# Second block's attention heads: the reciprocal softmax sums reach the head rows by DMA through DRAM instead of sixteen small products and a copy

## The reference, cut to what matters

```python
y = rmsnorm(h, norm_mix_g[l]) @ w_in[l]
q = partial_rotary(y[..., 0:512].reshape(B, S, 8, 64))
k = partial_rotary(y[..., 512:1024].reshape(B, S, 8, 64))
v = y[..., 1024:1536].reshape(B, S, 8, 64)
att = dilated_sliding_attention(q, k, v)      # softmax(q k^T / 8 + pattern) v, per head
conv = conformer_conv(...)                    # a convolution over 31 tokens, beside it
h = h + concatenate([att, conv]) @ w_out[l]
```

## Time and profile before

| | |
|---|---|
| median of three runs | 1579.19 us (1577.89 to 1580.6) |
| the profiled execution | 1579.18 us, its span 1576.9 us |
| PE busy | 1558.7 us, 99% of the span |
| DVE, ACT, POOL busy | 752.0, 627.4, 682.3 us |
| PE's granted clock | 0.99 of full speed over the whole, 1.00 in the stage of the change |
| attention stage, pairs 0 to 3 | 997.27 to 1046.21 us |

### The profile page before, as it was taken

One profiled execution on the slowest core, in us unless ns is written; L12 is line 12 of the kernel. 1 busy time (PEld: TensorE's weight loads), 2 busy tenths in 40 slices (PEclk: granted clock), 3 DMA queues, 4 the chain that ended last, 5 costly groups with the idle time before them and its releaser, 6 DMA issues.

```text
span 1576.9 us, 18796 instructions
## 1 busy us (share of the span) xinstructions
PE 1558.7 (99%) x7412; PEld 1261.0 (80%) x7412; DVE 752.0 (48%) x1295; ACT 627.4 (40%) x1135; POOL 682.3 (43%) x520
## 2 busy tenths in 40 slices
PE   9999999999999999999999999999999999999998
PEld 6888867788888888888888887568878888888886
DVE  6999523646666352133308698863432420022103
ACT  3534563543435333233332434673442542234322
POOL 1585333243544544454454454024413544444442
PEclk7999999999999999999999999999999999999999
DMA  9676532268534353333333442003213333333331
GB/s 319 139 110 154 134 81 80 54 227 281 202 104 134 110 171 126 96 98 94 105 109 99 135 120 81 14 28 94 81 40 94 102 99 97 103 89 99 96 104 68
DMA packets 221704, 180.28 MB, mean 114 GB/s; under 512 B 24232, under 2 KB 184360, under 8 KB 221488
## 3 DMA queue, kind: packets, MB, share of 16 engines
q1 hardware_dynamic: 214080, 166.68, 36.8%
q10 hardware_dynamic: 7536, 12.40, 2.2%
HBM read 172.49 MB, written 6.55 MB: 114 GB/s over the span
## 4 chain that ended last, share of the span: by engine, by line
PE 80%; ACT 1%; DVE 1%; POOL 0%; issue 0%; DVEq 0%; ACTq 0%
PE banks L647 13%; PE banks L648 13%; PE banks L653 13%; PE banks L729 9%; PE banks L730 9%; PE banks L734 9%; PE banks L776 3%; PE banks L759 1%; PE banks L760 1%; PE banks L761 1%; PE banks L1097 1%; PE banks L1110 1%; PE banks L1197 1%; PE banks L985 1%; PE banks L1183 0%; PE banks L1184 0%
## 5 line engine op out<-in xcount | busy, mean ns | idle before, releaser
L2564 POOL TENSOR_TENSOR w_lo<-raw,w_hi 128x512 fp32r<-128x512 f32 (+1 forms) x484 | 647.0, 1360 | 789.6 <-ACT w_hi L1267 788.8
L1267 ACT ACTIVATE w_hi<-raw 128x512 fp32r<-128x512 f32 (+1 forms) x484 | 275.9, 619 | 319.4 <-PE banks L734 244.7
L647 PE MATMUL banks<-h_hi,w_hi 128*128 128x512 f32 x936 | 367.1, 392 | 0.0
L648 PE MATMUL banks<-h_lo,w_hi 128*128 128x512 f32 x936 | 364.3, 389 | 0.0
L653 PE MATMUL banks<-h_hi,w_lo 128*128 128x512 f32 x936 | 250.2, 389 | 0.0
L647 PEld LDWEIGHTS banks<-h_hi,w_hi 128*128 128x128 f32 x936 | 175.7, 188 | 38.7 <-issue 2.4
L648 PEld LDWEIGHTS banks<-h_lo,w_hi 128*128 128x128 f32 x936 | 175.7, 188 | 36.6 <-issue 0.7
L653 PEld LDWEIGHTS banks<-h_hi,w_lo 128*128 128x128 f32 x936 | 175.7, 188 | 36.6
L2382 DVE SCALAR_TENSOR_TENSOR banks<-att_area,cols,banks 128x512 f32<-128x512 f32 x116 | 87.5, 754 | 3.4
L729 PE MATMUL banks<-w_hi,u_hi 128*128 128x512 f32 x224 | 87.1, 389 | 0.0
L730 PE MATMUL banks<-w_hi,u_lo 128*128 128x512 f32 x224 | 87.1, 389 | 0.0
(11 more groups left out here) (456 smaller groups left out, 2597.0 us busy)
## 6 DMA issues: line engine op xcount, KB each, us to landing
raw<-in_w_in SPq DMA_DIRECT2D x57, 512.0 KB, 4.2
raw<-in_w_ffn_up SPq DMA_DIRECT2D x44, 512.0 KB, 3.8
raw<-in_w_up SPq DMA_DIRECT2D x32, 512.0 KB, 4.0
raw<-in_w_down SPq DMA_DIRECT2D x32, 512.0 KB, 3.7
ada_ring<-in_w_ada SPq DMA_DIRECT2D x24, 512.0 KB, 5.7
raw<-in_w_ffn_down SPq DMA_DIRECT2D x20, 512.0 KB, 3.6
raw<-in_w_s_glu SPq DMA_DIRECT2D x16, 256.0 KB, 3.1
raw<-in_w_mlstm_down SPq DMA_DIRECT2D x8, 512.0 KB, 6.7
```

What stands on the lines that cost most here:

```text
L647: te.matmul(ps, wv[0][:, i, :], rh, start=(i == 0), stop=False)
L648: te.matmul(ps, wv[0][:, i, :], rl, start=False, stop=False)
L1267: sc.activation(W_HI[SLOT[key]][:, part_], raw[:, RAW_SLOT[key], part_], ACT.Copy).then_inc(*hi_set.up((key, n_)))
L2564: gp_.tensor_tensor(W_LO[s_][:, part_], raw[:, RAW_SLOT[key], part_], W_HI[s_][:, part_].bitcast(F32), ALU.subtract).then_inc(*lo_made.up( ...
```

## The change

The small products, their bank and ACT's copy go. The eight columns of reciprocals of a pair are written to a buffer in DRAM, ordered there as query tile, head of the pair, query, so that each element of 4 bytes goes to a place of its own. Two further transfers read them back, one for each head, 64 times over, each as four pieces of 512 bytes for each of 64 partitions. All three are issued by ACT: the first in step j = 0 of the pair, the two others in step j = 2, behind a wait of ACT for the landing of the first. DVE's `normalise` waits for the second of the two instead of for ACT's copy.

```diff
+        rd_d = nc.dram_tensor("att_rd_rows", (AT, TT, 2, P), F32, kind="Internal").ap()
...
-        r_mm, at_s, at_v, at_r = products("att_products_done", "r_row", "scores", "values", "rd_rows")
+        r_mm, at_s, at_v = products("att_products_done", "r_row", "scores", "values")
...
-        rd_row_out = signal("rd_row_out", AT)
+        rd_moved = signal("rd_rows_moved", [(p_, n) for p_ in range(AT) for n in ("out", "in0", "in1")], 16)
...
-            def rd_rows(p_):
-                ps = take("turn", ("rd", p_), rd_row_out[p_])
-                pe.wait_ge(*at_norm["rd", p_])
-                for i in range(TT):
-                    for h in (2 * p_, 2 * p_ + 1):
-                        r0 = 64 * (h % 2)
-                        last = te.matmul(ps[r0:r0 + 64, i * P:(i + 1) * P], att_rd(h, i).broadcast_to([P, 64]), ident[:, :], start=True, stop=True, tile_position=(0, r0))
-                last.then_inc(*at_r.up(p_))
...
-                rd_rows(p_)
                 att_values(p_, TT - 1)
...
-            def rd_row(p_):
-                act.wait_ge(*at_r[p_])
+            def rd_out(p_):
+                act.wait_ge(*at_norm["rd", p_])
+                sc.dma_start(rd_d[p_].rearrange("i s q -> q (i s)"), att_rd(2 * p_, 0, 2 * TT), allow_slow_non_contiguous=True).then_inc(*rd_moved.up((p_, "out")))
+
+            def rd_in(p_):
+                act.wait_ge(*rd_moved[p_, "out"])
                 if p_ >= 2:
                     act.wait_ge(*o_ls[p_ - 2])
-                sc.activation(scr[:, p_ % 2, :], ps_of(("rd", p_))[:, :], ACT.Copy).then_inc(*rd_row_out.up(p_))
+                for s_ in range(2):
+                    sc.dma_start(scr[64 * s_:64 * s_ + 64, p_ % 2, :].rearrange("p (i q) -> p i q", q=P), rd_d[p_, :, s_, :].partition_broadcast(64)).then_inc(*rd_moved.up((p_, f"in{s_}")))
...
                         values_hi(p_ - 1)
+                    if j == 0:
+                        rd_out(p_)
                     if j == 0 and p_ == AT - 1:
                         high_ahead("qkv", 2, KD - 2)
-                rd_row(p_)
+                    if j == 2:
+                        rd_in(p_)
...
             def normalise(p_):
                 dve.wait_ge(*at_v[p_, TT - 1])
-                dve.wait_ge(*rd_row_out[p_])
+                dve.wait_ge(*rd_moved[p_, "in1"])
                 ve.tensor_tensor(scr[:, p_ % 2, :], ps_of(("av", p_))[:, :], scr[:, p_ % 2, :], ALU.mult).then_inc(*at_norm.up(("normed", p_)))
```

## The result

The changed kernel takes 1594.45 us (median of four runs, 1593.08 to 1595.34) against 1578.54 us for the kernel before beside it: ratio 1.0094, 95% interval 1.0082 to 1.0106 (the plain quotient of the two medians is 1.0101). By the medians that is 15.9 us more where 2.9 us less were forecast, and it lies outside the range up to 1583.0. The side was that of the first rival, but further out.

The account below looks back on a forecast made before the run. PE was taken to bound the kernel: -3.5 us (small products) + 0.5 (first issue, pair 3) + 0.1 (small misses) = -2.9 us, from 1579.18 to 1576.3 us. Range 1575.2 to 1583.0 us.

Parts of the forecast that it names:

- the first rival: ACT's wait in front of the reads: slow write holds PE; 1582.3 us at a 6.7 us write; chance 0.20.
- What bounds the kernel: Attention: chain of waits all PE in pairs 0 to 2, leaving PE for ACT in pair 3; PE busy 1558.7 of 1576.9 us.
- What goes, 3.50 us: Small products on PE's chain, four times 0.87 or 0.88 us, vanish; the value product behind them stays at 0.86 us.
- The issues, 0.5 and 0.9 us of ACT's time: ACT: write's issue 0.5 us, hidden except in pair 3; two reads' issues 0.9 us, fitting; 0.1 us for small misses.
- How long the write takes, 3.7 us, at most 6.7: Write's landing: 2.0 us fixed plus 64 pieces per engine at 26 ns; upper bound used 74 ns; inside every budget.
- The budgets: Time from write's issue to latest landing PE doesn't notice: 5.7, 5.2, 5.2 and 4.7 us by pair, 20.8 in all.
- four times the excess: Price of a write landing later than the budgets, over four pairs; gain cancelled at 5.9 us, 1591 us total at 9.
- The reads, 2.1 to 2.9 us: Reads' landing before DVE's `normalise`, up to 0.6 us late against 1.1 us of slack; cost nothing, but near.
- rival 3: Reads land late, DVE becomes the limit: `normalise` 2.4 us late, 4.1 us together, 1580.4 us; chance 0.09.
- Rivals 2 and 4: Longer DMA issues on ACT, 1577.9 us, chance 0.11; small products hidden anyway, PE gains nothing, 1579.8 us, chance 0.02.
- rival 2: ACT: reads' issues take 0.5 us more, first issue 1.0 instead of 0.5; net about -1.3, 1577.9 us; chance 0.11.
- The gain reaches the end: Behind the attention PE has no DMA to wait for, so the whole 2.9 us gain reaches the span's end.

Follow-up runs that it names:

- floor kernel: Changed kernel without any spreading of the reciprocals (no small products, copy or transfers; values scaled by stale rows): 1576.19 us, ratio 0.998 to the kernel before.
- the one with spread pieces: Changed kernel with each 4-byte piece of the write in its own 512 bytes of DRAM, reads fetching a constant input: 1576.16 us, ratio 0.9976.

## Why the prediction was wrong, point by point

- **What bounds the kernel: right.** The attention was bound by PE in pairs 0 to 2. The floor kernel and the one with spread pieces show it by their gain of 3.1 and 3.3 us.
- **What goes, 3.50 us: mis-sized, 2.9 us.** I took the value product behind the small ones to stay at 0.86 us; it went back to 1.01 and more (2.05 for two).
- **The issues, 0.5 and 0.9 us of ACT's time: wrong in both.** The first costs nothing, not even in pair 3, which lasts 8.80 us both in the floor kernel, with no issue, and in the one with spread pieces, with it. ACT's queue runs ahead of ACT:

```profile
999.72 0.38 ACTq L1649 DMA_DIRECT2D att_rd_rows<-sm  x1
999.93 0.72 ACT L1637 ACTIVATE att_area<-att_area,sm 128x512 f32<-128x512 f32 x1
```

  This is ACT in order of time, pair 0 of the changed kernel: the write stands behind both exponentials of step 0 in the program, and its issue runs at 999.72, before the first of them starts, while ACT is still copying. So it isn't true, as the section on the time before has it, that ACT does nothing else while an issue lasts. The reads' issues took 1.25 to 1.5 us together, and there ACT does stand still; that this is because the queue had been held by the wait and had nothing ahead to hand over fits, but wasn't tested.
- **How long the write takes, 3.7 us, at most 6.7: the step that failed.** It landed in 9.0 us, and 8.4 to 9.5 with any number of neighbouring pieces. I multiplied 64 pieces per engine by 26 ns, a time per packet of larger pieces, and added 2.0. The packets took 7 ns each and were over within 0.8 us; nearly all of the 9 us came behind them. The bound "from above" wasn't one: its 74 ns was a mean over packets that were mostly far larger, and no price per packet bounds a time that passes behind the packets. The sentence that mattered stood in the first rival (neighbouring partitions write into the same 32 bytes), as a remark without a price. The rule of the Trainium skill ("DMA: Bandwidth & Descriptors", Specifications), that below 512 bytes the engine reads, modifies and writes, was a warning in the right direction. No run here shows the reading and modifying, and smallness alone isn't slow: 1024 separate pieces of 4 bytes land in 2.9 us. What in the neighbourhood of the pieces costs the time stays open.
- **The budgets: the form right.** With the issue as it really came (999.72) and 1.34 us of reads, pair 0's budget is 1008.62 - 999.72 - 1.34 - 0.1 - 0.6 = 6.9 us; the write's 8.97 less 6.9 is 2.1, and PE idled 2.10 us. But "four times the excess" left out the next point.
- **The reads, 2.1 to 2.9 us: mis-sized, 4.2 to 5.6 from issue to landing.** With the write late as well, rival 3 came on top of rival 1: DVE's `normalise` waited 3.4 to 9.3 us, and since the next pair's write stands behind it, the delays closed into a loop of 16.0 us a pair in pairs 0 and 1. I had treated the two rivals as separate, each with its own slack; with 9 us for the write, my formula gave 1591, and 1594.5 was measured.
- **Rivals 2 and 4.** The issues were longer, as rival 2 had it, but only the reads', 0.6 us each; the kernel with spread pieces has reads' issues of 0.5 to 0.6 us and reaches the floor all the same. That the small products were hidden is refuted by the floor kernel.
- **The gain reaches the end: right,** as the floor kernel and the one with spread pieces show (2.9 us less in the attention, 3.1 and 3.3 in the whole).

## What to carry to other kernels

A strided DMA store of single words isn't priced by its pieces: look at how close in DRAM its pieces lie. Here 16 bytes apart was enough (3.0 us, one landing), and so was turning the data first, so that a whole run goes to one place. Such a store also holds the transfers issued behind it, in its own queue and in another. When a step leaves a bound engine for a chain of transfers, add the chain up once around (write, wait, reads, consumer, the next round's first step) and compare it with the period, not each wait with its own slack. And an upper bound made from rows of another kind of transfer is no upper bound.

## What the hardware showed that I had not expected

- 128 stores of 4 bytes beside each other in DRAM took 8.4 us, 1024 stores of 4 bytes 512 bytes apart 2.9 us, and one run of 32 bytes from each of 128 partitions 1.4 us.
- The packets of 1024 stores were over within 0.8 us in both layouts; the landing came 7.4 us behind them when they lay beside each other, 1.2 us when they didn't.
- While such a write was under way, a load of 512 KB in SP's queue took 9.9 us instead of 4.4.
- The same write in the same program took 9.0 us in pairs 0 and 1 and 11.4 and 12.8 us in pairs 2 and 3 when no reads followed it. Not explained.
- ACT issued a DMA 0.2 us before an activation started that stands ahead of it in the program, beside another that was running.
- PE had no work for 2.10 us up to 1010.74, and was granted 0.50 of its clock from 1011.0 to about 1014.4 us. This cost next to nothing here, because another path of the same length, which didn't go through PE, set the time.
